# Even mixer: the causal convolution's 31 taps as column-tiled matrix products over shifted copies, with the query and key projection moved to the front

## The chip, the cores and the metric

The kernel runs on one core of one Trainium2 chip. The metric is the device time of one execution in microseconds: 1789.8 us, the median of three runs (1789.62, 1789.8 and 1793.51). The profile below is one execution with a span of 1786.5 us, from its first instruction to its last; 3.3 us lie between that span and the median of the runs.

The core has a matrix engine (PE, with its weight loads shown apart as PEld), two elementwise engines (DVE and ACT), a slow general engine (POOL) and a queue that issues most DMAs (SP). Every engine works through its own list of instructions in order and waits at semaphores for the others.

## The reference

Two stacks of layers run over one sequence of 256 tokens of width 1024. Feed-forward blocks stand around four mixers; the change is inside the first, the even mixer, which runs once:

```python
def even_mixer(h, w_in, w_out, conv_w, conv_b, ln_g, ln_b, q_g, k_g, sinks):
    proj = h @ w_in                              # 256 x 1792
    a_val, a_gate, q, k, v = jnp.split(proj, cuts, axis=-1)   # 512, 512, 512, 128, 128
    u = a_val * jax.nn.sigmoid(a_gate)
    u = lax.conv_general_dilated(u, conv_w[:, None, :], (1,), ((30, 0),), ...,
                                 feature_group_count=512) + conv_b
    u = jax.nn.silu(layer_norm(u, ln_g, ln_b))
    q, k = rms_norm(q, q_g), rms_norm(k, k_g)    # 8 query heads, 2 key heads of 64
    o = banded_attention(q, k, v, 127, sinks)
    return jnp.concatenate([u, o], axis=-1) @ w_out
```

The convolution is causal and depthwise: output t of a channel is the sum over 31 taps of weight k times input t - 30 + k of the same channel. Two tiles of 128 tokens are attended; each channel group j holds 128 of the 512 channels.

## The kernel before, in words

**Weights.** All weights arrive in a fixed list of units (`plan`), each up to 128 x 1024 float32. SP loads unit after unit into six staging buffers. ACT copies a unit to a high part `whi` (L1242), and DVE subtracts to get the low part `wlo` (L1740); there are four buffers of each. A product is then three matmuls, high by high, high by low and low by high (`three`, L596 to L598). SP may load unit u when DVE has split unit u - 6, and ACT may split it when PE has used unit u - 4. A weight unit of the even mixer costs PE 24 matmuls with 256 columns or 12 with 512.

**The even mixer.** Each engine's program is a set of generators that `weave` interleaves: one step of each per round, and each generator starts at its own round. `products` projects and then convolves, `swa` is the attention in turns (turn i issues the scores of pair i of heads, the transposes of pair i - 2 and the value products of pair i - 3), `down` multiplies by `w_out`, and `layer_norm` normalises the convolution's result over the channels (mean, variance and scale go over PE too). The order in each engine's list follows from the starting rounds alone; nothing is reordered at run time.

**The convolution.** 20 of the 31 taps are DVE instructions (L1749, one multiply-add of 128 x 256 per tap and channel group, in `conv`). The other 11 are PE products with diagonal 128 x 128 weights, which ACT writes (L1425). They are plain float32 products of 256 columns (L882), and every such product is two instructions, for the low and the high half of the weights. DVE adds the two sums (L2082). Each channel group's input `ev_u` comes out of a short chain: DVE scales the two projections (L2050), ACT takes a tanh (L1411), DVE combines (L1749).

**Order on PE.** Gate and value columns of groups 0 and 1 first, then queries, keys and values, then groups 2 and 3; then heads are transposed (L784), and 8 steps of taps stand between turns of the attention (scores L842, transposes L829, value products L816). The mean of the normalisation is L917, the transposed attention output L796, the variance L926, the scale row L935. The low half of the normalised part, `ev_ml` (L2130 on DVE), is needed by the fifth of the eight `down` units.

Of the kernel before, what the change touches and what calls it, by code (L numbers as in the profile page):

```python
# [10 lines left out]
ALU = mybir.AluOpType  # L11
# [5 lines left out]
S = 256  # L17
# [9 lines left out]
PE_TAPS = 11  # L27
# [5 lines left out]
def _consts():  # L33
# [29 lines left out]
    put("rcount", np.broadcast_to(rc.reshape(1, -1), (128, 64)))  # L63
    first = np.concatenate(parts, axis=1)
# [139 lines left out]
def build(nc, A, out):  # L204
    ctx = ExitStack()
    with ctx:
# [203 lines left out]
        class Even:  # L410
            def __init__(self, c):
# [8 lines left out]
                self.taps = sb("ev_taps", [128, 4, PE_TAPS, 128], c=c)  # L420
# [8 lines left out]
                self.cwr = sb("ev_cwr", [34, 512], c=c)  # L429
# [3 lines left out]
                self.cw = sb("ev_cw", [128, 4, 34], c=c)  # L433
# [127 lines left out]
        def tensor_program(e):  # L561
# [288 lines left out]
            def even(m):  # L850
# [3 lines left out]
                def products():  # L854
                    for j0 in (0, 2):
                        ps = [room(("ev u", j0 + j)) for j in range(2)]
                        yield from tiles(g, [b[:, 0:256] for b in ps], 256, 4)
                        second = tiles(g, [b[:, 256:512] for b in ps], 256, 4, [("ev u mm", j0)])
                        next(second)
                        yield  # L860
                        next(second)
                        if not j0:
                            row(g)
                        yield
                        for j in range(2):
                            done("ev u", j0 + j)
                        if not j0:
                            heads = x_cols(g, 0, 512)
                            next(heads)
                            conv_weights()  # L870
                            yield
                            yield from heads
                            yield from x_cols(g, 512, 256)

                    for j0 in (0, 2):
                        ps = room(("ev tap", j0))
                        for j in (j0, j0 + 1):
                            e.wait_ge(*K.at("ev u", j))
                            for k in range(PE_TAPS):
                                if k % 6 == 0:  # L880
                                    e.wait_ge(*K.at("ev tap", j, k // 6))
# [3 lines left out]
                                if k + 1 == PE_TAPS and j % 2:  # L885
                                    w.then_inc(*K.inc("tap_mm", ("ev tap mm", j0)))
                                if k % 6 == 5 or k + 1 == PE_TAPS:
                                    yield
                        done("ev tap", j0)

                def conv_weights():
                    ps = room(("ev cw",))
                    e.wait_ge(*K.at("par", g))
                    for j in range(4):
                        w = e.transpose(ps[:, j * 34:(j + 1) * 34], m.cwr[:, j * 128:(j + 1) * 128], ident[0:34, 0:34])
# [43 lines left out]
                weave([(1, products()), (11, swa()), (27, down(g, m.rows)), (24, layer_norm())])  # L939
# [286 lines left out]
        def scalar_program(e):  # L1226
# [172 lines left out]
            def even(m):  # L1399
# [3 lines left out]
                def products():  # L1403
                    for j0 in (0, 2):
# [7 lines left out]
                        if j0:  # L1412
                            return

                        yield from x_cols(512)
                        by_token(g, 0, 512, lambda t: m.qkv[:, t, 0:512].rearrange("p (i j e) -> p j i e", i=4, j=2),
                                 src=lambda ps: ps.rearrange("p (j i e) -> p j i e", j=2, i=4))
                        yield from x_cols(256)
                        by_token(g, 512, 256, lambda t: m.qkv[:, t, 512:768])

                def diagonals():
                    e.wait_ge(*K.at("ev ch"))
                    for j in range(4):
                        for k in range(PE_TAPS):
                            w = e.activation(m.taps[:, j, k, :], ident, ACT.Copy, scale=m.cw[:, j, k:k + 1])  # L1425
                            last = k % 6 == 5 or k + 1 == PE_TAPS
                            w.then_inc(*K.inc("tap", *([("ev tap", j, k // 6)] if last else [])))
                            if last:
                                yield

                def layer_norm():
# [5 lines left out]
                    for j in range(4):  # L1437
                        e.activation(m.sq[:, j, :], m.acc[:, j, :], ACT.Silu, scale=m.cw[:, j, 32:33],
                                     bias=m.cw[:, j, 33:34]).then_inc(*K.inc("ln_silu"))
# [1316 lines left out]
```

## Time and profile before

| | us |
|---|---|
| median of three runs | 1789.8 |
| span of the profiled execution | 1786.5 |
| PE busy | 1772.1 (99%) |
| DVE busy | 1266.1 (71%) |
| ACT busy | 947.8 (53%) |
| even mixer, from its first transpose to the next block's | 190.49 to 297.55, 107.1 |

Busy time is the union of an engine's instructions. PE's instructions overlap (the next one starts before the last one's result is out), so the cost of one in a stream is the distance between starts and not its own duration. "Idle before" is what the engine stood still for, with the instruction that released it.

### The profile page before, as it was taken

Reading aid. Unit: us, or ns where it says so; the run is one execution under the profiler, and the core shown is the slowest. Engines: PE = TensorE matmul, PEld = TensorE weight load, DVE = VectorE, ACT = ScalarE, POOL = GpSimd, SP = SyncE. Lnnn points to the kernel's source line nnn. Section 1 sums busy time; section 2 is a strip of 40 time slices with the busy share of each in tenths; the row PEclk is TensorE's granted clock in tenths of the full one; section 3 lists DMA queues with packets and bytes.
Section 4 is the critical chain, followed back from the end, with each engine's and each line's share of the span. In section 5 each row is a group of like instructions: output and inputs, shape, how many; then the busy total and the mean of one; then the engine's idle time right before and its main releaser. Section 6 shows DMA issues by size and latency. Waiting matters only on the chain.

```text
span 1786.5 us, 24871 instructions
## 1 busy us (share of the span) xinstructions
PE 1772.1 (99%) x9702; PEld 1508.5 (84%) x9702; DVE 1266.1 (71%) x1893; ACT 947.8 (53%) x1348; POOL 30.2 (2%) x39
## 2 busy tenths in 40 slices
PE   9999999999999999999999999999999999999998
PEld 8888888888888888888888788888888878888887
DVE  7774795876577657677656977777755878677774
ACT  6554655554555546555545535455545544555553
POOL 0000000000000001000000000000000000000000
PEclk9999999999999999999999999999999999999999
DMA  8656523666666655466655544556555443456653
GB/s 271 193 180 201 178 72 118 189 177 205 180 193 183 195 177 181 116 196 184 198 169 180 179 130 130 178 181 189 192 193 173 141 155 126 150 188 193 188 195 109
DMA packets 227677, 309.24 MB, mean 173 GB/s; under 512 B 22558, under 2 KB 176318, under 8 KB 227562
## 3 DMA queue, kind: packets, MB, share of 16 engines
q1 hardware_dynamic: 227398, 307.35, 55.1%
q8 instruction: 78, 1.28, 0.3%
q10 hardware_dynamic: 164, 0.30, 0.0%
q14 instruction: 37, 0.30, 0.0%
HBM read 306.57 MB, written 1.05 MB: 172 GB/s over the span
## 4 chain that ended last, share of the span: by engine, by line
PE 92%; DVE 5%; ACT 2%; issue 1%; POOL 0%; POOLq 0%; ACTq 0%; DVEq 0%
PE ps L645 26%; PE ps L596 15%; PE ps L598 15%; PE ps L597 15%; PE ps L647 13%; DVE wlo L1740 1%; PE ps L1144 1%; PE ps L608 1%; PE ps L816 1%; PE ps L842 1%; DVE ev_acc L1749 1%; PE ps L829 1%; ACT whi L1242 1%; PE ps L784 0%; DVE m_scr L1749 0%
## 5 line engine op out<-in xcount | busy, mean ns | idle before, releaser
L1740 DVE TENSOR_TENSOR wlo<-staging,whi 128x1024 fp32r<-128x1024 f32 (+1 forms) x580 | 692.6, 1210 | 339.0 <-ACT whi L1242 338.4
L1242 ACT ACTIVATE whi<-staging 128x1024 fp32r<-128x1024 f32 (+1 forms) x580 | 606.5, 1050 | 477.2 <-PE ps L598 293.7
L645 PE MATMUL ps<-hT,whi 128*128 128x512 f32 x1984 | 624.1, 396 | 0.2 <-DVE wlo L1740 0.2
L647 PEld LDWEIGHTS ps<-hT,wlo 128*128 128x128 f32 x1984 | 372.7, 188 | 88.1
L647 PE MATMUL ps<-hT,wlo 128*128 128x256 f32 x1984 | 389.8, 278 | 0.0
L645 PEld LDWEIGHTS ps<-hT,whi 128*128 128x128 f32 x1984 | 302.1, 189 | 0.4 <-DVE wlo L1740 0.4
L596 PE MATMUL ps<-whi,fh 128*128 128x512 f32 x504 | 196.1, 389 | 0.0
L597 PE MATMUL ps<-wlo,fh 128*128 128x512 f32 x504 | 196.1, 389 | 0.0
L598 PE MATMUL ps<-whi,fl 128*128 128x512 f32 x504 | 196.1, 389 | 0.0
L596 PE MATMUL ps<-whi,hT 128*128 128x512 f32 (+3 forms) x464 | 184.8, 398 | 0.8 <-DVE wlo L1740 0.6
L598 PE MATMUL ps<-whi,hT 128*128 128x512 f32 (+3 forms) x464 | 177.4, 382 | 0.0
L597 PE MATMUL ps<-wlo,hT 128*128 128x512 f32 (+3 forms) x464 | 177.1, 382 | 0.0
L598 PEld LDWEIGHTS ps<-whi,fl 128*128 128x128 f32 x504 | 94.6, 188 | 19.7
L597 PEld LDWEIGHTS ps<-wlo,fh 128*128 128x128 f32 x504 | 94.6, 188 | 19.5
L596 PEld LDWEIGHTS ps<-whi,fh 128*128 128x128 f32 x504 | 94.6, 188 | 19.4
L596 PEld LDWEIGHTS ps<-whi,hT 128*128 128x128 f32 x464 | 87.2, 188 | 21.4 <-issue 3.8
L598 PEld LDWEIGHTS ps<-whi,hT 128*128 128x128 f32 x464 | 87.2, 188 | 16.2
L1313 ACT ACTIVATE fh<-sg 128x512 fp32r<-128x512 f32 x62 | 39.2, 632 | 114.0 <-DVE sg L1844 114.0
L597 PEld LDWEIGHTS ps<-wlo,hT 128*128 128x128 f32 x464 | 87.4, 188 | 14.3 <-issue 0.5
L1829 DVE TENSOR_TENSOR sg<-sg,R 128x512 f32<-128x512 f32 x124 | 85.8, 692 | 4.3
L1826 DVE TENSOR_TENSOR sg<-ps,sg 128x512 f32<-128x512 f32 x124 | 84.8, 684 | 0.2
L596 PE MATMUL ps<-hT,whi 128*128 128x256 f32 x288 | 82.8, 287 | 0.0
(347 smaller groups left out, 1900.6 us busy)
## 6 DMA issues: line engine op xcount, KB each, us to landing
staging<-in_w_in SPq DMA_DIRECT2D x92, 512.0 KB, 3.3
staging<-in_ffn_w_gate SPq DMA_DIRECT2D x84, 512.0 KB, 4.2
staging<-in_ffn_w_up SPq DMA_DIRECT2D x84, 512.0 KB, 4.5
staging<-in_ffn_w_down SPq DMA_DIRECT2D x84, 512.0 KB, 4.1
staging<-in_w_ffn_gate SPq DMA_DIRECT2D x44, 512.0 KB, 4.5
staging<-in_w_ffn_up SPq DMA_DIRECT2D x44, 512.0 KB, 4.6
staging<-in_w_ffn_down SPq DMA_DIRECT2D x44, 512.0 KB, 4.2
staging<-in_od_w_in SPq DMA_DIRECT2D x16, 512.0 KB, 3.7
```

Source lines behind the costliest of these rows:

```text
L596: e.matmul(o, lh, rh, start=start, stop=False)
L597: e.matmul(o, lh, rl, start=False, stop=False)
L598: return e.matmul(o, ll, rh, start=False, stop=stop)
L608: w = e.transpose(ps[:, t * 128:t * 128 + 128], xs[:, t, k * 128:k * 128 + 128], ident)
L645: e.matmul(o, wh[:, kk, j * 128:j * 128 + 128], hT[:, k, :], start=k == 0, stop=False)
L647: m = e.matmul(o[:, 0:256], wl[:, kk, j * 128:j * 128 + 128], hTh[:, k, :], start=False, stop=k == KD - 1)
L816: w = e.matmul(ops[t][:, (h0 + j) * 64:(h0 + j) * 64 + 64], a.pt[i % 2][:, o:o + 128], a.vN(kt, h0 + j), start=kt == 0, stop=kt == t)
L1242: e.activation(high(u)[:, 0:n], stage[u % NS][:, 0:n], ACT.Copy).then_inc(*K.inc("hi", ("hi", u)))
L1313: e.activation(f.fh[:, 2 * p:2 * p + 2, :], s[:, :, 0:256], ACT.Copy).then_inc(*K.inc("fh", ("fh", g, p, 0)))
L1740: e.tensor_tensor(low_of(u)[:, 0:n], stage[u % NS][:, 0:n], high(u)[:, 0:n].bitcast(F32), ALU.subtract).then_inc(*K.inc("lo", ("lo", u)))
L1826: e.tensor_tensor(ss, PS[:, b:b + 2, 0:256], ss, ALU.add).then_inc(*K.inc("ps_r", *[("ev", u) for u in users]))
L1829: e.tensor_tensor(ss, ss, R22, ALU.mult).then_inc(*K.inc("ps_r", ("scaled", g, p, part)))
```

## The change

All 31 taps go to PE, as 8 steps of 4 taps. A product has 32 output channels and contracts over 128 rows: four shifted copies of the 32 channels, stacked on the partitions. Four such products, with 32 columns of weights each, fill the array side by side; each writes its own 32 partitions of the sum. The shifted copies (`u4`) and the weights' taps (`wv`) are laid out by DMAs between SBUF partitions, and DVE multiplies the taps with a constant folded identity to get the weights (`w4`). Queries, keys and values are projected first, so the attention starts at round 7 and lies between the projections of `u` and not between taps only.

```diff
@@ plan_even @@
+            plan_cols(ev, 1024, 512)
+            plan_cols(ev, 1536, 256)
             for c in (0, 256):
                 plan_cols(ev, c, 256)
                 plan_cols(ev, 512 + c, 256)
-                if c == 0:
-                    plan_cols(ev, 1024, 512)
-                    plan_cols(ev, 1536, 256)
@@ PE, products @@
+                    e.wait_ge(*K.at("ev w4"))
                     for j0 in (0, 2):
                         ps = room(("ev tap", j0))
-                        for j in (j0, j0 + 1):
-                            e.wait_ge(*K.at("ev u", j))
-                            for k in range(PE_TAPS):
...
-                                w = e.matmul(ps[:, 256 * (j % 2):256 * (j % 2) + 256], m.taps[:, j, k, :],
-                                             m.u[:, j, PAD - (CONV_W - 1) + k:][:, 0:S], start=k == 0,
-                                             stop=k == PE_TAPS - 1)
+                        e.wait_ge(*K.at("ev u4", j0))
+                        for n in range(2 * STEPS):
+                            j, k = j0 + n // STEPS, n % STEPS
+                            c = 256 * (n // STEPS)
+                            for q in range(GROUPS):
+                                w = e.matmul(ps[32 * q:32 * q + 32, c:c + 256], m.w4[:, q, j, k, :],
+                                             m.u4[:, j, q, 4 * k:4 * k + S], start=k == 0, stop=k == STEPS - 1)
...
+                            if n + 1 in (6, 11, 16):
+                                yield
@@ PE @@
-                weave([(1, products()), (11, swa()), (27, down(g, m.rows)), (24, layer_norm())])
+                weave([(1, products()), (7, swa()), (23, down(g, m.rows)), (22, layer_norm())])
@@ ACT: diagonals() is gone @@
-                            w = e.activation(m.taps[:, j, k, :], ident, ACT.Copy, scale=m.cw[:, j, k:k + 1])
@@ DVE, conv @@
-                        for k in range(PE_TAPS, CONV_W):
...
-                                    w = stt(m.acc[:, j, :], src, m.cw[:, j, k:k + 1], m.acc[:, j, :], ALU.mult, ALU.add)
+                    e.wait_ge(*K.at("ev wv"))
...
+                    for q in range(GROUPS):
+                        e.tensor_tensor(m.w4[:, q, :, :, :].rearrange("p j k c -> p (j k) c"), fold,
+                                        m.wv[:, q, :, :].rearrange("p j k -> p (j k)").unsqueeze(2).broadcast_to(
+                                            [128, 32, 32]), ALU.mult).then_inc(
...
+                            e.tensor_scalar(m.acc[:, j, :], bk("ev tap", j0)[:, c:c + 256], m.cb[:, j, 0:1], None,
+                                            ALU.add).then_inc(
@@ SP @@
+            def taps_load(m):
+                e.wait_ge(*K.at("ev taps"))
+                load("ev_wv", *[(m.wv[quarters[k], q, :, :], m.cwt[quarters[q], k, :, :])
+                                for k in range(GROUPS) for q in range(GROUPS)], steps=[("ev wv",)])
+
+            def shifted_load(m, j0):
+                e.wait_ge(*K.at("ev pad"))
+                e.wait_ge(*K.at("ev u", j0 + 1))
+                n = S + 4 * (STEPS - 1)
+                load(f"ev_u4_{j0}", *[(m.u4[quarters[k], j0:j0 + 2, q, 0:n], m.u[quarters[q], j0:j0 + 2, 1 + k:1 + k + n])
+                                      for k in range(GROUPS) for q in range(GROUPS)], steps=[("ev u4", j0)])
...
+            before = {first[1] + 10: (even_load, evs), first[1] + 14: (taps_load, evs),
+                      first[1] + 18: (shifted_load, evs, 0), first[2]: (shifted_load, evs, 2), first[4] + 10: (odd_load, ods),
```

The list of SP, from the last small parameter of the even mixer to the next block's weights (`ev_w_in` and `ev_w_out` are weight units; `x16` is sixteen DMAs). Before:

```order
L2639 DMA ev_sk<-in_ev_sinks 128x8
L2695 DMA staging<-in_ev_w_in 128x4x256 x4
L2695 DMA staging<-in_ev_w_out 128x1024 x8
L2695 DMA staging<-in_ffn_w_gate 128x4x256 x2
L2695 DMA staging<-in_ffn_w_up 128x4x256 x2
```

Changed:

```order
L2621 DMA ev_sk<-in_ev_sinks 128x8
L2692 DMA staging<-in_ev_w_in 128x4x256 x4
L2621 DMA ev_wv<-ev_cwt 32x32 x16
L2692 DMA staging<-in_ev_w_out 128x1024 x4
L2621 DMA ev_u<-ev_u 32x2x284 x16
L2692 DMA staging<-in_ev_w_out 128x1024 x4
L2621 DMA ev_u<-ev_u 32x2x284 x16
L2692 DMA staging<-in_ffn_w_gate 128x4x256 x2
```

Three batches of sixteen DMAs now stand among the weight units (`ev_u<-ev_u` writes the shifted copies `ev_u4`), and the last two wait for DVE's `ev_u`.

The list of PE at the first taps. `L842` and `L846` are the same line, the attention's scores, before and after. Before:

```order
L882 MATMUL ps<-ev_u,ev_taps 128x256 [waits s_tap,s_ev_u,s_in_act]
L882 MATMUL ps<-ev_u,ev_taps 128x256 x5
L842 MATMUL ps<-ev_kT,ev_qT 128x128 [waits s_in_act,s_heads]
L842 MATMUL ps<-ev_kT,ev_qT 128x128
L882 MATMUL ps<-ev_u,ev_taps 128x256 [waits s_tap]
L882 MATMUL ps<-ev_u,ev_taps 128x256 x4
L842 MATMUL ps<-ev_kT,ev_qT 128x128 [waits s_heads]
```

Changed (value products L820, transposes L833):

```order
L846 MATMUL ps<-ev_kT,ev_qT 128x128 [waits s_pt,s_att_mx]
L846 MATMUL ps<-ev_kT,ev_qT 128x128
L886 MATMUL ps<-ev_u,ev_w 32x256 [waits s_ev_u4_0,s_att_mx,s_conv]
L886 MATMUL ps<-ev_u,ev_w 32x256 x23
L820 MATMUL ps<-ev_qkv,ev 128x64 [waits s_pt]
L820 MATMUL ps<-ev_qkv,ev 128x64
L833 MATMUL ps<-cst,ev 128x128 [waits s_exp,s_att_mx]
L833 MATMUL ps<-cst,ev 128x128
L846 MATMUL ps<-ev_kT,ev_qT 128x256 [waits s_att_mx,s_pt]
L846 MATMUL ps<-ev_kT,ev_qT 128x256
L886 MATMUL ps<-ev_u,ev_w 32x256 x20
```

The first taps stood before the first scores; now they stand behind the scores of turn 3, ahead of those of turn 4, and start with a wait for the first batch of shifted copies. There are six steps of 24, 20, 20, 24, 20 and 20 products.

The list of DVE where the second pair of channel groups is made (`ISA` is the attention's masked score, one pair of heads; a second row of it reads its maximum). Before:

```order
L2021 ISA ev<-ps,cst,ev_skp,ev_hr 128x128 [waits s_att]
L2021 ISA ev 128x1
L2021 ISA ev<-ps,cst,ev_skp,ev_hr 128x128
L2021 ISA ev 128x1
L1749 SCALAR_TENSOR_TENSOR ev_acc<-ev_u,ev_cw,ev_acc 128x256 [waits s_conv] x6
```

Changed:

```order
L1730 TENSOR_TENSOR wlo<-staging,whi 128x1024 [waits s_hi]
L2011 ISA ev<-ps,cst,ev_skp,ev_hr 128x256 [waits s_att]
L2011 ISA ev 128x1
L2011 ISA ev<-ps,cst,ev_skp,ev_hr 128x256
L2011 ISA ev 128x1
L2045 TENSOR_TENSOR ev_th<-ps,R 128x512 [waits s_prod]
L2045 TENSOR_TENSOR ev_th<-ps,R 128x512
L1739 SCALAR_TENSOR_TENSOR ev_u<-ev_th 128x256 [waits s_ev_tanh] x2
L1969 TENSOR_TENSOR ev<-ev 128x8 [waits s_exp]
```

The multiply-adds between the turns are gone, and `ev_u` of groups 2 and 3 now stands behind the masked scores of turn 4 (the first with 256 columns).

## Rows read from the trace of the kernel before

**Rows 1.** The page: busy time, share of the span, instructions.

```profile
PE 1772.1 (99%) x9702; PEld 1508.5 (84%) x9702; DVE 1266.1 (71%) x1893; ACT 947.8 (53%) x1348; POOL 30.2 (2%) x39
```

**Rows 2.** Windows of the even mixer: length, busy time, granted clock, DMA share, GB/s.

```profile
190.50:233.30 42.80, 42.67 (x312) 40.21 (x313) 38.68 (x72) 35.94 (x79) 5.10 (x4) 1.00 0.54 169
233.30:274.70 41.40, 38.86 (x236) 32.00 (x235) 35.72 (x100) 19.19 (x55) 0.00 (x0) 1.00 0.13 39
```

**Rows 3.** What PE waited for, 190 to 298 us: total, times, longest.

```profile
PE ps L816 <- ACT ev L1381: 0.7, 1, 0.7
```

**Rows 4.** Groups by line, DVE, 208 to 266 us: count, busy, mean ns, idle.

```profile
L1749 DVE SCALAR_TENSOR_TENSOR ev_acc<-ev_u,ev_cw,ev_acc 128x256 f32<-128x256 f32 x76 | 31.5, 478 | 0.0
```

**Rows 5.** Groups (first row) and timeline of PE: start, duration, line, operands.

```profile
L882 PE MATMUL ps<-ev_u,ev_taps 128*128 128x256 f32 x88 | 21.0, 387 | 0.0
...
250.40 0.55 PE L816 MATMUL ps<-ev_qkv,ev 128*128 128x64 f32 x4
250.78 0.39 PE L829 MATMUL ps<-cst,ev 128*128 128x128 f32 x2
251.10 0.70 PE L842 MATMUL ps<-ev_kT,ev_qT 64*128 64x256 f32 x4
251.74 2.43 PE L882 MATMUL ps<-ev_u,ev_taps 128*128 128x256 f32 x10
254.00 0.55 PE L816 MATMUL ps<-ev_qkv,ev 128*128 128x64 f32 x4
```

**Rows 6.** Timeline of PE's weight loads: full array, then 32-row tiles.

```profile
233.21 1.12 PEld L784 LDWEIGHTS ps<-cst,ev_qkv 128*128 128x128 f32 x10
...
1016.09 0.52 PEld L1144 LDWEIGHTS ps<-m_scr 32*128 32x128 f32 x8
```

**Rows 7.** Windows: four units of `ev_u` projection, four units of `down`.

```profile
221.79:233.31 11.52, 11.52 (x98) 11.52 (x97) 11.33 (x21) 11.43 (x31) 4.24 (x2) 1.00 0.55 180
...
286.50:297.50 11.00, 10.93 (x48) 9.07 (x49) 7.58 (x8) 4.17 (x4) 0.00 (x0) 1.00 0.89 265
```

**Rows 8.** Timeline of PE, then of DVE: the heads' transposes, and `ev_u`.

```profile
233.31 1.25 PE L784 MATMUL ps<-cst,ev_qkv 128*128 128x128 f32 x10
...
239.47 1.28 DVE L2050 TENSOR_TENSOR ev_th<-ps,R 128x512 f32<-128x512 f32 x2
240.67 0.99 DVE L1749 SCALAR_TENSOR_TENSOR ev_u<-ev_th 128x256 f32<-128x256 f32 x2
```

**Rows 9.** SP's timeline (start, duration of issue), then DMAs: count, size, us to landing.

```profile
200.27 0.60 SPq L2639 DMA_DIRECT2D ev_qg<-in_ev_q_norm_g  x1
214.77 0.34 SPq L2695 DMA_DIRECT2D staging<-in_ev_w_out  x1
...
out<-staging SPq DMA_DIRECT2D x1, 256.0 KB, 2.1
od_qg<-in_od_q_norm_g SPq DMA_DIRECT2D x2, 0.2 KB, 3.5
```

**Rows 10.** Timeline: PE at the end of the attention and normalisation, then DVE.

```profile
268.21 1.89 PE L917 MATMUL ps<-ev_acc,cst 128*128 128x256 f32 x8
272.12 1.06 PE L796 MATMUL ps<-cst,ev_o 128*128 128x128 f32 x8 [1.17 <-DVE ev_o L1996]
273.01 1.84 PE L926 MATMUL ps<-cst,ev_sqc 128*128 128x1 f32 x16
277.55 0.60 PE L935 MATMUL ps<-dg,cst 128*128 128x128 f32 x4
...
285.21 1.22 DVE L2130 TENSOR_TENSOR ev_ml<-ev_sqc,ev_mh 128x1024 fp32r<-128x1024 f32 x1
```

**Rows 11.** Windows after PE's last matmuls, start at 1780.04 and earlier.

```profile
1780.00:1782.00 2.00, 0.43 (x2) 0.01 (x1) 1.81 (x4) 1.12 (x4) 0.00 (x0) 1.00 0.58 238
...
1784.00:1785.00 1.00, 0.00 (x0) 0.00 (x0) 0.00 (x0) 0.00 (x0) 0.00 (x0) 0.81 0.80 299
1785.00:1786.00 1.00, 0.00 (x0) 0.00 (x0) 0.00 (x0) 0.00 (x0) 0.00 (x0) 0.50 0.60 225
```

More of the change, by code:

```diff
@@ L26 @@
 CONV_W = 31
-PE_TAPS = 11
+GROUPS = 4
+STEPS = 8
 PAD = 32
@@ L63, in _consts @@
     put("rcount", np.broadcast_to(rc.reshape(1, -1), (128, 64)))
+    put("fold", np.arange(128)[:, None] % 32 == np.arange(32)[None, :])
     first = np.concatenate(parts, axis=1)
@@ L854, in products @@
                 def products():
+                    heads = x_cols(g, 0, 512)
+                    for _ in range(3):
+                        next(heads)
+                        yield
+                    next(heads)
+                    row(g)
+                    yield
+                    yield from heads
+                    keys = x_cols(g, 512, 256)
+                    next(keys)
+                    conv_weights()
+                    yield
+                    yield from keys
                     for j0 in (0, 2):
@@ L857, in products @@
                         yield from tiles(g, [b[:, 0:256] for b in ps], 256, 4)
[L858 to L864, printed above, removed]
+                        yield from tiles(g, [b[:, 256:512] for b in ps], 256, 4, [("ev u mm", j0)])
                         for j in range(2):
@@ L1458, in swa @@
                     transposed("swa", 4, m.mh[:, 4:8, :])
-                weave([(1, products()), (10, swa()), (6, diagonals()), (27, down(m.rows)), (24, layer_norm())],
-                      catch_up)
+                weave([(1, products()), (6, swa()), (23, down(m.rows)), (22, layer_norm())], catch_up)
             def odd(m):
@@ L2038, in products @@
                 def products():
+                    for n in range(4):
+                        side.due += 1
+                        if n == 1:
+                            diag(g)
+                        if n == 3:
+                            row(g)
+                        yield
+                    conv_weights()
+                    yield from x_cols(256)
                     for j0 in (0, 2):
@@ L2041, in products @@
                             side.due += 1
-                            if half == 1 and not j0:
-                                diag(g)
-                            if half == 3 and not j0:
-                                row(g)
                             yield
@@ L2079, in add_first @@
+                    for j0, rounds in ((0, 5), (2, 3)):
+                        for _ in range(rounds):
+                            yield
                         e.wait_ge(*K.at("ev tap mm", j0))
                         for j in (j0, j0 + 1):
-                            e.wait_ge(*K.at("conv", j, CONV_W - 1))
-                        e.tensor_tensor(m.acc[:, j0:j0 + 2, :], m.acc[:, j0:j0 + 2, :], two(bk("ev tap", j0)),
-                                        ALU.add).then_inc(
-                            *K.inc("conv", ("ev", ("ev tap", j0)), *([("ev conv",)] if j0 else [])))
@@ L2147, in swa @@
                     transposed("swa", 4, m.mh[:, 4:8, :], m.ml[:, 4:8, :])
-                weave([(11, swa()), (1, products()), (5, conv()), (27, down(g, m.rows, 1.0)), (24, layer_norm())],
+                weave([(7, swa()), (1, products()), (9, conv()), (23, down(g, m.rows, 1.0)), (22, layer_norm())],
                       catch_up)
@@ L2651, in even_load @@
                      (m.sk[:, :], A["ev_sinks"].broadcast_to([128, 8])), steps=[("par", m.g)])
+            quarters = [slice(32 * q, 32 * q + 32) for q in range(GROUPS)]
+            def taps_load(m):
[8 more added lines that the diff above has]
+                                      for k in range(GROUPS) for q in range(GROUPS)], steps=[("ev u4", j0)])
             def odd_load(m):
@@ L2711, in sync_program @@
                 if u in before:
-                    stage_load, m = before[u]
-                    stage_load(m)
+                    stage_load, *m = before[u]
+                    stage_load(*m)
                 unit(u)
```

100 lines of the change are left out of this document (34 added, 66 removed).

## The prediction, made before the changed kernel ran

> **What bounds the kernel now.** First the busy times: PE works 99% of the span [rows 1], so only time that PE saves or stands still for can move the end. Then the windows of the even mixer: PE is busy 42.7 of 42.8 us while it projects, and 38.9 of 41.4 us while attention, taps and normalisation alternate [rows 2]. Then the waits: of the idle time in the middle part 0.7 us [rows 3] and 1.2 us [rows 10] have a releaser worth the name, both in the tail of the attention. The changed code therefore has about 2.5 us of idle PE to recover, and everything else must come from cheaper PE work. DVE's 76 multiply-adds, 31.5 us [rows 4], are the largest piece of work that goes, but PE hardly waits for them; nor does it for ACT's weight copies.
>
> **PE work that goes and comes.** A tap step before: ten instructions for five taps of 256 columns start at 251.74, and the next line starts at 254.00 [rows 5]. Of these 2.26 us 0.1 is the first weight load, which nothing hides behind the scores (0.103 us, see [rows 6] below); (2.26 - 0.1) / 10 = 0.216 us each. 88 instructions [rows 5] are 19.0 us.
>
> After: 128 products, 256 instructions of the same 256 columns. What four of them cost when they stand in four column tiles is what the case turns on, and no row shows column tiles. The nearest row is row tiles. Eight loads of 32-row weights, which alternate between two row tiles, take (0.52 - 0.19) / 7 = 0.047 us each; ten loads for the whole array take (1.12 - 0.19) / 9 = 0.103 us each, at the same 128 moving columns [rows 6]. So two tiles do run at once, and that although each product's low and high half follow one another in the list: the second tile's low half starts before the first tile's high half. If column tiles behave alike and all four run at once, the taps are 256 / 4 x 0.216 = 13.8 us. If two run at once they are 27.6 us, if none does 55.3 us. I take four at once, since the nearest row shows as many tiles at once as it has.
>
> A step of another tile shape than its neighbour's costs PE a drain: the scores' four instructions last from 251.10 to 251.74 where two overlapping pairs of 0.216 us would be 0.43 [rows 5], 0.2 us for going in. I give each of the six tap steps 0.3 us, 1.8 us in all. PE work then changes by -19.0 + 13.8 + 1.8 = **-3.4 us**.
>
> The Trainium skill, in "TensorE: Matmul & The Clock Gate", part 3 "Packing small matmuls", gives a measured 2.38 times for three column tiles, says that matmuls start and end strictly in the order of the list, and that a weight load is pulled ahead of running matmuls only when the row group differs. Rows 6 speak against the strict order, for row tiles. By that rule a column tile's high half would hold back the next tile's low half, and only two products would overlap, as in the second rival below.
>
> **When the first shifted copies are there.** The product units are the same ones, only their order changes; before, the last of them ends at 233.3 [rows 7]. Now the transposes of the heads (234.40 - 233.31 = 1.1 us, [rows 8]), four scores of 0.42 (the row's 0.63 is for twice the columns), two transposes of 0.32 and a value product of 0.39 [rows 5] lie in front of that point: PE reaches the first tap at 233.3 + 3.8 = 237.1. The last unit for groups 0 and 1 ends four units earlier (11.5 us, [rows 7]), at 221.8. Behind it come the transposes of the heads 1.1, one unit 2.9 and the first scores 0.4: 226.2. DVE's list then has a low part, two masked scores (0.7) and `ev_u` (239.47 to 241.66, 2.2 us [rows 8]); with the low part's wait for ACT I come to 229.7.
>
> SP then issues sixteen DMAs. One small DMA among others takes 0.60 us to issue, one large one that stands alone 0.34 [rows 9]; with 0.04 between them that bounds a batch of sixteen (fifteen distances) by 5.7 and 9.6 us. I take 0.55 each, nearer to the small ones: 8.3 us. From the last issue to landing are 2.1 to 3.5 us [rows 9]; I take the middle, 2.8. Copies: 229.7 + 8.3 + 2.8 = 240.8, and PE stands still from 237.1 for **3.7 us**. The batch of tap weights before it is issued while DVE still has its old work, and PE does not wait for it.
>
> **When the second ones are there.** This is a chain through four queues. `ev_u` of groups 2 and 3 stands on DVE behind the masked scores of turn 4, which PE issues only behind the first tap step: 240.8 + 24 products (6 x 0.43 + 0.3 = 2.9) + value product, transposes and scores (1.3) = 245.0; masked scores 1.1 and `ev_u` 2.2 = 248.3; sixteen DMAs 8.3 and 2.8 = 259.4. On PE lie two tap steps of 2.45, three pieces of attention of 1.3 to 1.6, and 1.6 us of waiting for ACT, whose copy and exponentials stand behind the tanh: PE is there at 254.4 and stands still for **5.0 us**.
>
> **The tail.** From 259.4: three tap steps 2.9 + 2.45 + 2.45, attention between them 2.0 + 1.4 + 1.4, to 272.0; the last value product with ACT's copy before it (0.7, as in [rows 3]) 1.8; the output's scaling and transposes 1.7, as 0.8 and 0.9 ([rows 10], 272.12 to 273.01); the mean 1.7: 277.2, where the first `down` unit starts. Before, the last taps end at 262.2 and the variance, which now comes one unit later, ends at 274.7 [rows 10]. Unit 2.7, variance 1.7, unit 2.7: the scale row starts at 284.3. From it to the end of `ev_ml` were 286.4 - 277.55 = 8.9 us [rows 10] over DVE, ACT and DVE again. Three `down` units (8.2 us) covered that; now only two (5.4 us) do, because `layer_norm` starts one round before `down` and not three rounds. `ev_ml` is there at 293.2, a wait of **3.4 us** for PE in place of 0.3. Four more units of 2.73 [rows 7] end the mixer at 304.1, against 297.55.
>
> **The sum.** -3.4 us of work, +3.7, +5.0 and +3.1 of new waits, and small ones that cancel (1.6 for ACT behind the tanh, less 2.5 of idle time that goes with the old order; the walk's own rest is -0.9): +6.6 us. Outside the mixer nothing changes; the units of the next block are loaded long before. The profiled execution would have a span of 1786.5 + 6.6 = 1793.1, and with the 3.3 us between span and median the time is **1796.4 us**.
>
> **The rivals.**
>
> *Two products at a time.* For it: the list's order, low and high half of one tile behind each other, and that no row shows more than two tiles at once. The first tap step grows by 2.5 us, and so does the second batch's arrival; the next two hide in the wait that is there anyway; the last three grow by 6.7. Together +6.6 + 2.5 + 6.7 = +15.8: 1805.6 us.
>
> *None at a time.* For it: rows 6 are row tiles, another direction of the array. 55.3 us of taps, of which the second wait's 5.0 us hide nearly all: +6.6 + (55.3 - 13.8) - 5.0 - 2 = +41: 1831 us.
>
> *Not slower.* Its one mechanism is the speed of the two batches of DMAs between SBUF partitions. At 0.34 + 0.04 us an issue and 2.1 us to land, the copies come at 237.5 and, down the same chain, at 252.6. PE waits 0.4 and 1.7 us instead of 3.7 and 5.0, and the end moves by -6.8: 1789.6 us. The sum turns at about 0.38 us an issue. Against it: the small DMAs of the same queue took 0.60 [rows 9]. If the tap steps also cost less to enter than I say and the waits for ACT go with DVE's lighter list, it would be 1784.
>
> *The clock falls in a wait.* PE's granted clock was 1.00 until 1784 and 0.50 from 1785 on, with no matmul since 1780.4: it fell after some 4 us of idle [rows 11], from 2.4 to 1.2 GHz. The waits of 3.7 and 5.0 us are of that size. Every microsecond of taps behind them that runs at the lower level takes two: with a step and its attention (4.2 us) behind each wait, up to +8, I take +4: 1800 us. [...]
>
> **How the numbers follow.** A difference of under 0.3% (5.4 us) counts as no change. Four at a time 0.44: 1796.4, own range 1790 to 1802, of which 0.27 is slower and 0.17 the same. Two at a time 0.25, none 0.06, the clock on top of four at a time 0.05: all slower. Not slower 0.20, of which 0.08 the same and 0.12 faster. Slower 0.63, same 0.25, faster 0.12. The range leaves out the case of none (0.06), the half of "not slower" that gains most and the upper end of two at a time: 1786 to 1812 holds about 0.83.
>
> **What would show it.** The group of tap products: 256 instructions; in a step of 24 products the starts of a round of four lie 0.43 us apart if four run at once, 0.86 if two do, 1.7 if none. PE's waits must name the two DMAs of shifted copies, with 3 to 4 and about 5 us, and DVE's `ev_ml` with about 3 us. SP's rows must show sixteen issues in about 9 us, twice, the second starting 18 to 20 us after the first. DVE's time falls by some 25 us without any effect on the end. The windows between the waits must show a granted clock of 1.00. The forecast is wrong if PE waits under 2 us for both batches together, if a round of four costs more than 0.6 us, or if PE's idle time shows up at the projections, where the tap weights' batch holds SP and DVE.

## The result and the profile after

The changed kernel takes **1805.1 us** (median of 4 runs, 1804.2 to 1805.9), the kernel before 1789.7 (4 runs): 1.0087 times as long, 95% interval 1.0075 to 1.0099. The forecast was 1796.4 with a range of 1786 to 1812. The sign and the range held; of the 15.4 us, the likeliest case had only 6.6.

The mixer itself, from one normalisation's first transpose to the next one's. Timeline of TensorE, before and after (start, duration, line, operands):

```profile
190.49 0.74 PE L608 MATMUL ps<-cst,xs 128*128 128x128 f32 x5
...
297.55 0.71 PE L608 MATMUL ps<-cst,xs 128*128 128x128 f32 x5
```

```profile
192.07 1.07 PE L612 MATMUL ps<-cst,xs 128*128 128x128 f32 x8
...
315.15 1.03 PE L612 MATMUL ps<-cst,xs 128*128 128x128 f32 x8
```

107.06 us became 123.08: **+16.0 us**. The other 1.5 us between the spans (1786.5 and 1804.0) lie ahead of the mixer, where the two programs are the same. There the granted clock of TensorE was low for a while in this execution and stood at 1.00 over the same four microseconds in the kernel before (window, all engines, of the changed kernel):

```profile
9.00:13.00 4.00, 3.61 (x17) 3.47 (x18) 3.80 (x6) 3.64 (x9) 0.00 (x0) 0.57 1.10 368
```

The traces of runs 4, 6, 9 and 10 below have the same low stretch, the others don't, so times of two kernels can differ by some 1.5 us that no edit made. All that the change itself does is in these 123 us. What TensorE waited for there (total, times, longest), where before only two were worth the name, 0.7 us [rows 3] and 1.2 us [rows 10]:

```profile
PE ps L886 <- DMA ev_u<-ev_u: 10.3, 2, 6.2
PE ps L600 <- DVE ev_ml L2111: 3.0, 1, 3.0
PE ps L820 <- ACT ev L1385: 1.4, 2, 0.8
PE ps L800 <- DVE ev_o L1986: 0.9, 1, 0.9
```

The three waits of the forecast are there: for the first and the second copies, and for `ev_ml`. What the rows of waits don't show is what came behind them. The timeline of the six tap steps (48 instructions are 24 products, 40 are 20):

```profile
243.32 5.13 PE L886 MATMUL ps<-ev_u,ev_w 128*32 128x256 f32 x48 [4.14 <-DMA ev_u<-ev_u]
249.83 2.37 PE L886 MATMUL ps<-ev_u,ev_w 128*32 128x256 f32 x40
...
265.00 4.53 PE L886 MATMUL ps<-ev_u,ev_w 128*32 128x256 f32 x48 [6.20 <-DMA ev_u<-ev_u]
271.58 2.37 PE L886 MATMUL ps<-ev_u,ev_w 128*32 128x256 f32 x40
```

Undisturbed, 40 instructions last 2.30 us from their first start to the next line's, and 48 last 2.73 (in runs 1 and 8 below), so six rounds cost 0.43 us more than five: a round of four products costs 0.43 us, as one product did before [rows 5], and going into a step costs 0.14. The steps behind the two waits took 5.06 and 4.46 us by the same measure. The windows of TensorE (length, busy time, granted clock, DMA share, GB/s) say why:

```profile
241.00:243.00 2.00, 0.00 (x0) 0.57 0.47 115
243.00:248.00 5.00, 4.68 (x45) 0.50 0.99 366
...
249.00:250.00 1.00, 1.00 (x11) 1.00 0.00 0
...
265.00:268.00 3.00, 3.00 (x30) 0.50 0.99 327
268.00:269.00 1.00, 1.00 (x20) 0.71 0.15 43
270.00:272.00 2.00, 2.00 (x22) 1.00 0.00 0
282.00:285.00 3.00, 3.00 (x12) 0.54 0.00 0
303.00:306.00 3.00, 3.00 (x8) 0.50 0.78 232
```

The granted clock fell from 1.00 to 0.50 (2.4 to 1.2 GHz) four times, and not once in the mixer before [rows 2]: in both waits for copies, in the attention's tail, and in the wait for `ev_ml`. Note also the DMA share of 0.99 in the same windows: what made the steps slow is not settled by these rows alone.

And the chain, behind which the second wait stands (start, duration, what):

```profile
241.09 2.09 DMA ev_u<-ev_u
243.32 5.13 PE ps L886 x48
248.45 0.59 PE ps L820 x4
249.04 0.23 PE ps L833 x2
249.26 0.66 PE ps L846 x4
249.95 1.02 DVE ev L2011 x4
250.97 1.21 DVE ev_th L2045 x2
252.20 0.43 ACT ev_th L1420
252.65 0.44 DVE ev_u L1739
253.15 0.60 SPq L2621
...
262.74 2.13 DMA ev_u<-ev_u
265.00 4.53 PE ps L886 x48
```

It is the chain of the forecast, link by link: copies, first step, scores, masked scores, `ev_u`, sixteen issues, landing. So whatever lengthens the first step also delays the second batch. The issues (min, median and max in ns behind the count, then the first and the last start) follow one another 0.64 us apart. The first batch takes 10.2 us and the second 9.6, and not 8.3:

```profile
L2621 SPq DMA_DIRECT2D ev_u<-ev_u x32: 596/597/1106, 230.9 to 262.7; - x32
```

### The profile page after: what moved, and what is told of

Read it like the earlier page. It is cut to its first block, busy times and chain, and to the rows that moved or that the text cites. A ratio compares the mean times of both kernels' runs of the same rounds, so it can differ in the third digit from the quotient of the medians.

```text
span 1804.0 us, 25136 instructions
## 1 busy us (share of the span) xinstructions
PE 1775.9 (98%) x9870; PEld 1505.8 (83%) x9870; DVE 1241.2 (69%) x1819; ACT 935.4 (52%) x1304; POOL 30.3 (2%) x40
## 4 chain that ended last, share of the span: by engine, by line
PE 93%; DVE 3%; SPq 1%; ACT 1%; issue 1%; DMA 1%; POOLq 0%; POOL 0%; ACTq 0%; DVEq 0%
PE ps L649 26%; PE ps L600 16%; PE ps L602 15%; PE ps L601 15%; PE ps L651 13%; PE ps L612 1%; PE ps L1148 1%; SPq L2621 1%; PE ps L820 1%; DVE wlo L1730 1%; PE ps L846 1%; PE ps L886 1%; PE ps L833 1%; PE ps L788 1%; DVE m_scr L1739 0%
```

## The experiments

Eleven runs, all variants of the changed kernel, timed against the kernel before on the same chip (1788.6 to 1789.5 us there). The changed kernel's own 1805.1 us was taken once, beside 1789.7, so a difference to it is one across chips; the mixer's length in the trace, taken as above, is the finer measure. The numbers in brackets are the range of the runs, the ratio to the kernel before, and its 95% interval.

### 1. TensorE kept busy in the waits

```
  ps = room(("ev tap", j0))
+ for _ in range(13 if j0 else 9):
+     e.matmul(ps[:, 0:256], C("ones"), cst[:, 0:256], start=True, stop=True)
  e.wait_ge(*K.at("ev u4", j0))
```

> Ahead of the two waits for the shifted copies TensorE multiplies constants into the bank that the taps then overwrite: 9 products of 256 columns (18 instructions at 0.216 us, 3.9 us) ahead of the first, 13 (5.6 us) ahead of the second. The copies can land no sooner by it. Theory A (the waits of 4.2 and 6.2 us drop the granted clock to 0.5 and the first tap step behind each runs at the lower level): the granted clock stays 1.00 from 238 to 272 us, both first steps of 48 instructions take 2.75 us in place of 5.06 and 4.46, and what follows the second batch is as far behind it as before: 2.3 + 1.7 = 4.0 us less, 1801. Theory B (those two steps are slow for another reason: the share of the DMA engines, at 1.0 just then, slows TensorE's reads of SBUF, or the first round of taps is slow by itself): 48 instructions still take 4.5 to 5 us, and the time stays at 1805 or rises by what the fillers run over.

Measured: 1799.3 us (1797.9 to 1802.2; 1.0056, interval 1.0041 to 1.0071), the mixer 117.3 us. Timeline of the two steps, and the windows that hold them:

```profile
241.23 2.80 PE L888 MATMUL ps<-ev_u,ev_w 128*32 128x256 f32 x48
...
260.48 2.80 PE L888 MATMUL ps<-ev_u,ev_w 128*32 128x256 f32 x48 [0.31 <-DMA ev_u<-ev_u]
```

```profile
241.00:244.00 3.00, 2.93 (x50) 1.00 0.89 317
256.00:260.00 4.00, 4.00 (x20) 1.00 0.47 114
260.00:264.00 4.00, 3.69 (x56) 1.00 0.86 265
```

Theory A. Both steps fall by 2.33 and 1.73 us, with the DMA share nearly as high as before (0.89 and 0.86 in place of 0.99): the clock made them slow, not the traffic. Work that computes nothing made the kernel 5.8 us faster. 4.1 of these are the two steps; the rest, some 1.7 us, is in the tail, where the mean's eight instructions now took 1.54 us and not 2.65: here the clock stayed up, though the tail's waits of 0.7 and 0.9 us were the same. Behind the wait for `ev_ml`, where nothing filled in, it fell as before.

### 2. Nobody waits for the copies

```
- e.wait_ge(*K.at("ev u4", j0))
+ e.wait_ge(*K.at("ev pad"))
+ e.wait_ge(*K.at("ev u", j0 + 1))
- ... m.u4[:, j, q, 4 * k:4 * k + S], ...
+ ... m.u[:, j, 4 * k:4 * k + S], ...
```

> The tap products read ev_u itself where they read its shifted copies, so they wait only for ev_u; all 32 copies are still issued, and nobody waits for them. It leaves out the shift of the three other taps of each product. Theory A (the loss lies in the two waits for DMAs and the clock that they cost): the waits of 4.2 and 6.2 us and the slow steps (2.3 and 1.7 us) go, 14.4 us in all: 1791. What stays against the kernel before is then the wait for ev_ml with its own fall of the clock, 3.0 and 1.8 us, the same in the tail, 1.4 us, less 3.4 us of cheaper taps. Theory B (the new order of the projections is dear by itself, since attention now alternates with the u products and has no cover later): the waits move to DVE's masked scores and ACT's exponentials, and the time is above 1797.

Measured: 1789.0 us (10 runs, 1787.3 to 1790.0; 0.9999, interval 0.9990 to 1.0008). Theory A: the two waits and what hangs on them are nearly the whole slowdown. By time it is 16.1 us; by the mixer, which shrinks from 123.1 to 108.5, it is 14.6, where 14.4 were expected, and the other 1.5 us lie at the start of the program. The 3.0 us for `ev_ml` and the lower clock in the tail and behind it stay, and the cheaper taps balance them but for 1.4 us. No new wait of size shows that the order of the projections costs anything by itself.

### 3. Tile by tile

```
- for q in range(GROUPS):                      # k outside: tiles alternate
+ for i in range(GROUPS * n, GROUPS * n + GROUPS):
+     half, q, k = i // 32, i // STEPS % GROUPS, i % STEPS   # tile outside
```

> The same 128 tap products, but the eight steps of one column tile follow one another (tile outermost) where the four tiles alternated. Theory A (neighbours in the list run at once only if they stand in different column tiles): a product costs its whole 0.43 us, and the taps 128 x 0.43 = 55 us in place of 14.7. The first step grows by 7.5 us, the next two by 12.4 of which the second wait takes up 6.2, the last three by 20, less some 2 for a clock that no longer falls in a second wait: +31 us, 1836. Theory B (TensorE looks far enough ahead to fill the idle tiles from further down the list, or the tiles never were what made it fast): a step stays at 2.3 to 3 us and the time at 1805.

Measured: 1825.3 us (1825.2 to 1825.6; 1.0199, interval 1.0184 to 1.0214): slower than with alternating tiles by 20.2 us, where 31 were expected. Timeline of the steps at full clock:

```profile
254.76 7.15 PE L886 MATMUL ps<-ev_u,ev_w 128*32 128x256 f32 x40
263.29 7.15 PE L886 MATMUL ps<-ev_u,ev_w 128*32 128x256 f32 x40
272.04 8.88 PE L886 MATMUL ps<-ev_u,ev_w 128*32 128x256 f32 x48
```

Four products more cost 1.73 us, 0.43 each: neighbours in the same tile do follow one another. But 20 products would be 8.6 us and took 7.08, 24 would be 10.4 and took 8.81. Both steps change tiles twice, and each change saves 0.8 us, the time of two products. In the trace instructions follow 0.216 us apart until, 6 ns after the thirteenth of the sixteen of a tile, one more starts: the next tile's first. Four of either then run side by side. So theory A holds for neighbours, and B is right in that TensorE looks ahead, by about two products. The twelve changes of tile save 9.6 us, and that is most of the 11 us that the expectation missed; the other 1.7 us are the tail, which ran at the full clock here.

### 4. The projections in the old order

```
  plan, TensorE, ScalarE, VectorE: u (0, 1), heads, keys, u (2, 3), as before
- if n + 1 in (6, 11, 16): yield
+ if n % 4 == 3: yield
- weave([(1, products()), (7, swa()), (23, down(...)), (22, layer_norm())])
+ weave([(1, products()), (11, swa()), (27, down(...)), (24, layer_norm())])
```

> The new taps, but with the projections in the order of the kernel before (u of groups 0 and 1, heads, keys, u of groups 2 and 3), attention four rounds later as before, and the taps in eight steps of 16 products. Theory A (the copies' delay is what costs, not the tap products): the first copies land some 5 us before TensorE wants them; the second u is there at about 236, its copies at 236 + 16 x 0.64 + 2.1 = 248.3, and TensorE is there at about 245: one wait of 3 to 4 us, at most a short fall of the clock behind it. With 3.4 us of cheaper taps and the usual three rounds between mean and the first W_out product, so that ev_ml is not waited for: 1790, within 1787 to 1794. Theory B (taps in column tiles cost more than they save, or alternate badly with attention): above 1797 whatever the order.

Measured: 1798.3 us (1797.2 to 1801.5; 1.0046, interval 1.0029 to 1.0062). Neither theory: it is 8 us above A, and though the time is B's, the tap products didn't cost more. In the trace, which is of the slowest of the four executions, TensorE waited 6.7 us for the second copies and 4.1 us for `ev_qkv`, the scaled keys. The chain that ends in the keys:

```profile
232.57 0.60 SPq L2624
233.21 4.52 DMA staging<-in_ev_w_out
237.76 1.06 ACT whi L1247
238.85 1.23 DVE wlo L1734
240.07 0.34 DVE ev_qkv L2125
```

I had counted what the sixteen issues hand over late, and not what stands behind them in SyncE's list. A load of `W_out` weights goes out when the batch is done, at 233.2; its splitting stands on ScalarE and VectorE ahead of the keys' scaling, although the keys have nothing to do with it; and TensorE waits for the keys. `ev_u` of groups 2 and 3 was done at 248.4 and not at about 236, since it stood behind masked scores that waited for TensorE.

### 5 to 7. One cause at a time

```
e5  - for k in range(GROUPS) for q in range(GROUPS)]   (SyncE)
    + for k in range(2) for q in range(GROUPS)]        (SyncE), k = 2, 3 on GpSimd, behind its head norms
e6  - weave([(7, swa()), (1, products()), (9, conv()), ...        (VectorE)
    + weave([(1, products()), (7, swa()), (9, conv()), ...
e7  - (22, layer_norm())      on TensorE, ScalarE, VectorE; conv's rounds (0, 5), (2, 3)
    + (20, layer_norm())                                                 (0, 5), (2, 2)
```

> Of each sixteen DMAs of shifted copies SyncE issues eight and GpSimd, which has nothing else to do then, the other eight. Theory A (the copies are late because one queue needs 0.64 us for each of sixteen issues): if GpSimd issues as fast, a batch is issued in 5.1 us, the first copies are there at 230.9 + 5.1 + 2.1 = 238.1, before TensorE wants them, so the wait of 4.2 us goes and with it the slow first step, 2.3 us. The second batch is shorter by 5.1 us: 1.1 us of its 6.2 us stay, too short for the clock to fall, which gives 1.7 us more. 13.3 us less than 1805.1: 1792. Theory B (GpSimd needs twice as long for an issue, or the landing of the copies is what takes long): at 1.3 us an issue nothing is gained, 1805, and above it more is lost.

Measured: 1791.1 us (10 runs, 1790.4 to 1793.1; 1.0010, interval 1.0001 to 1.0019). The first wait is gone, of the second 1.4 us are left, and the clock stays up in the taps and in the tail. It falls behind `ev_ml`, where it now costs 2.9 us in place of 1.7. The mixer takes 109.7 us, 13.3 less, as expected. GpSimd issues one every 0.53 us (rows as for SyncE above):

```profile
L2590 POOL DMA_DIRECT2D ev_u<-ev_u x16: 536/536/712, 229.5 to 248.7; - x16
```

> Only VectorE's order changes: in each round what belongs to the products (the low part, the scaling of u) stands ahead of attention's masked scores, so ev_u of groups 2 and 3 no longer waits for the scores that TensorE issues behind the first tap step. Theory A (that order is why the second batch is late): u is there at 238.0 + 2.7 = 240.7; SyncE ends the first batch at 241.7, issues four loads of weights (2 us) and then the second, which lands at 243.8 + 10.2 + 2.1 = 256.1; TensorE wants it at 258.1. The wait of 6.2 us and the slow step behind it (1.7 us) go, the first wait of 4.2 us stays: 1797. Theory B (the second batch is bound by something else, the queue or the landing): the wait only shrinks by the 2 to 3 us between the two batches, 1802, or the scores come later and attention pays: 1805.

Measured: 1794.6 us (1793.5 to 1796.2; 1.0030, interval 1.0019 to 1.0042). The second wait is gone, and its slow step; of the two waits for copies one is left:

```profile
242.70 5.35 PE L886 MATMUL ps<-ev_u,ev_w 128*32 128x256 f32 x48 [3.73 <-DMA ev_u<-ev_u]
...
257.16 2.80 PE L886 MATMUL ps<-ev_u,ev_w 128*32 128x256 f32 x48
```

> The layer norm starts two rounds earlier (round 20, three before W_out's first product, as in the kernel before), so the mean stands ahead of the last value product and the scale row one unit earlier. Theory A (ev_ml was waited for since only two units lay between scale row and its first use): three units, 8.2 us, cover 8.9 us of DVE and ACT: the wait of 3.0 us shrinks to 0.7 and the clock does not fall behind it (1.8 us); the mean's products also fill the wait for ACT's last exponentials, up to 1.4 us. 5.5 us less: 1799.6. Theory B (the mean or the variance now wait themselves, for the taps' bias on DVE and the squares on ACT): the wait moves and at most 2 us are gained, 1803 or more.

Measured: 1799.6 us (1798.7 to 1801.3; 1.0057, interval 1.0044 to 1.0071). `ev_ml` costs 0.2 us in place of 3.0, the clock doesn't fall behind it, and TensorE's waits for ACT and DVE in the attention go from 2.5 to 2.1 us.

Theory A in all three runs, with 0.9 us under, 2.4 us under and 0.0 us off the time expected. That the last one met its time to the tenth is in part luck: in its trace the first wait was 0.6 us longer than in the changed kernel, and the two slow steps together 1.2 us shorter (4.3 and 4.1 us).

### 8. All three

> The changed kernel with all three edits of the last runs: two queues, the second u earlier, the mean earlier. Theory A (the loss is nothing but the two waits for the copies, the wait for ev_ml and the clock behind the three; the taps themselves are 3 to 4 us cheaper than before): the run in which nobody waited for copies took 1789.0, and the earlier mean takes 5.5 us off that: 1783.5, within 1782 to 1786, faster than the kernel before (1789.5). Theory B (the edits compete: GpSimd and SyncE issue at the same time, VectorE's square, bias and masked scores crowd in the last rounds): 1788 or more.

Measured: **1783.8 us** (6 runs, 1782.5 to 1785.8; 0.9970, interval 0.9958 to 0.9982): faster than both. Timeline of the mixer's ends, then all that TensorE waited for in it, then two windows:

```profile
190.39 0.84 PE L612 MATMUL ps<-cst,xs 128*128 128x128 f32 x6
...
291.43 0.82 PE L612 MATMUL ps<-cst,xs 128*128 128x128 f32 x6
```

```profile
PE ps L800 <- DVE ev_o L1987: 1.2, 1, 1.2
PE ps L887 <- DMA ev_u<-ev_u: 0.4, 1, 0.4
PE ps L600 <- DVE ev_ml L2112: 0.2, 1, 0.2
```

```profile
237.00:275.00 38.00, 36.42 (x403) 1.00 0.33 107
275.00:291.00 16.00, 15.76 (x70) 1.00 0.60 177
```

The mixer takes 101.0 us, 6.0 less than before and 22.0 less than in the changed kernel, with the same 256 tap instructions. The granted clock is 1.00 in all of it. That may not be so in each execution: run 7's trace has the same wait of 1.2 us for `ev_o`, and there the clock fell behind it and cost 1.6 us.

### 9 and 11. The old order of projections with the queues mended

e9 is e4 with the edits of e5 and e6. e11 moves GpSimd's first eight issues ahead of the head norms.

> The projections in the old order with the new taps once more (1798.3 in the run before), with the two queues and VectorE's order (u ahead of the masked scores). In that run's trace TensorE waited 4.1 us for the keys, since SyncE issued a batch of copies until 233.2 us and W_out's loads, whose splitting stands ahead of the keys on ScalarE and VectorE, came only then; and 6.7 us for the second copies. Theory A (both waits come from SyncE's sixteen issues and VectorE's order, not from the order of the projections): W_out's loads go out 5 us sooner, the keys' wait shrinks to 1 us or none; the second copies are issued from 239 on and land at 246, before TensorE wants them; the two steps at the lower clock (3.57 in place of 1.87 us) go: 3.1 + 6.7 + 3.4 = 13.2 us less, 1785. Theory B (with u first attention has less cover, whatever the queues do): the keys' wait stays over 3 us or attention's waits grow in the tail: 1790 or more.

Measured: 1789.8 us (10 runs, 1787.9 to 1794.0; 1.0004, interval 0.9995 to 1.0014), which is B's time within 0.2 us but not its place. The keys' wait is gone, the second copies are in time, but now the first ones are late by 4.1 us: in GpSimd's list they stand behind the square root for the keys.

> As the last run with u first (1789.8, a wait of 4.1 us for the first copies), but GpSimd issues its eight first copies ahead of the square roots of the head norms and not behind them. In the trace of that run its list held them back: the root for the keys ended at 234.4, eight issues until 238.2, landing at 240.1. Theory A (that list is all that was left): the issues start at 223 with ev_u, the copies are there by 231, the wait of 4.1 us and the lower clock behind it (0.6 us in the first, 0.7 us in the second step) go: 1784.4, as fast as the other order with its three edits (1783.8). Theory B (the roots are now late in turn: they wait behind eight issues of 0.53 us, and heads and keys with them): the wait moves to the transposes of the heads and over 2 us of the 5.4 stay: 1786.5 or more.

Measured: 1787.9 us (10 runs, 1786.1 to 1791.6; 0.9997, interval 0.9987 to 1.0007). The first wait is gone and 2.2 us of waiting for the second copies have come in its place, with a step at the lower clock behind it:

```profile
PE ps L888 <- DMA ev_u<-ev_u: 2.2, 1, 2.2
```

Theory B's time, but not its place: nothing moved to the heads. I don't count the old order as worse by nature. As far as it was taken it does as well as the kernel before and some 4 us worse than the new order with its edits, and each repair brought up the next wait.

### 10. One tile of four

```
- for q in range(GROUPS):
+ for q in range(1):
```

> The changed kernel with only one of the four products of each tap round, 32 products in place of 128; it leaves out three quarters of the convolution. Theory A (four column tiles run wholly at once): a round of one product takes as long as one of four, 0.43 us, and the steps keep their 2.3 and 2.7 us; the time stays at 1805, within 2 us. Theory B (the four share something, the issue of instructions or the reading of moving columns, so that the round of eight instructions is bound by 8 x 0.054): a round of two instructions is shorter, down to 0.11 us, the first and the last three steps shrink by up to 7 us in all, and the time falls to 1798 or less.

Measured: 1804.3 us (1803.8 to 1805.6; 1.0082, interval 1.0065 to 1.0099). Timeline:

```profile
254.69 2.35 PE L886 MATMUL ps<-ev_u,ev_w 128*32 128x256 f32 x10
```

10 instructions last as long (2.35) as the 40 of the changed kernel (2.37), and with three quarters of the tap products gone the mixer is as long as in the changed kernel (123.1 us). Three of four products are free: four column tiles run wholly at once.

## Why the prediction was partly right

**Point by point.** Mixer, predicted and measured:

| Term | Predicted | Measured |
|---|---|---|
| a round of four products | 0.43 us | 0.43 us |
| going into a tap step | 0.3 us | 0.14 us |
| tap work | -3.4 (19.0 to 15.6) | -5.3 (19.9 to 14.6) |
| wait for the first copies | +3.7 | +4.1 |
| wait for the second copies | +5.0 | +6.2 |
| wait for `ev_ml` (0.3 before) | +3.1 | +2.7 |
| lower clock | 0 | +7.4 |
| small ones | -1.8 | +0.9 (the rest) |
| sum | +6.6 | +16.0 |

The lower clock is 2.3 and 1.7 us in the two steps, 0.6 and 1.1 us in the tail (the output's transposes took 1.47 in place of 0.90 us, the mean 2.65 in place of 1.54, against run 1), and 1.7 us behind `ev_ml` (nine instructions in 3.71 us, where 0.23 each would be 2.04).

The taps after are 2 x 2.73 + 4 x 2.30 = 14.6 us at the full clock. Before, the eight steps were about 4 x 2.70 + 4 x 2.27 = 19.9 us by the same measure. The forecast's 19.0 left out what going into each of them costs (0.1 us) and counted it for the new steps, so its saving was 0.9 us too small for that alone.

**The step that failed is the term for the clock**, which the forecast put at 0 in the likeliest case and at 4 us in a rival with a chance of 0.05. It had the row for it: the clock fell after some 4 us without a matmul at the end of the span [rows 11]. Three terms of its own sum were waits of 3.1 to 5.0 us. With such rows, the fall belonged to the likeliest case and the steady clock to the rival. It also asked only what runs slowly behind a wait for copies and passed over the wait for `ev_ml` and the tail. Run 1 shows the two steps' part by itself, 4.1 us. The 1.7 us of the tail also went in that run, but they went without an edit in run 5 too, so they are not the fillers' doing for certain.

The Trainium skill says in "TensorE: Matmul & The Clock Gate", part 1, that an idle engine loses the full clock and has to work before it gets it back. The waits of this trace agree: in the first one the clock was at 0.50 by 242 us, and it was back at 1.00 by 249, after 5 us of tap products.

**Smaller misses.** The small terms were off by 2.7 us. TensorE's waits for ACT and DVE, without `ev_ml`, are 2.6 us where they were 2.5: the old order's idle time, which the forecast let go, was still there in the tail, and the wait behind the tanh (1.0 us, forecast 1.6) came on top. The remaining -0.9 was a rest of the walk without a cause of its own, and the trace doesn't have it. Two of the forecast's signs also failed: the second batch started 22 us after the first and not 18 to 20, and the windows between the waits show a clock of 0.50 until 248.

**A rival had the time and not the cause.** "Two products at a time" gave 1805.6, 0.5 us from the measured 1805.1. Its sign was a round of 0.86 us. The round took 0.43, and run 10 shows that four products cost what one does. Had only the time been looked at, the wrong rival would have been taken for shown. The range held with luck, too: its upper end was there for this rival and not for the clock, whose own rival ended at 1800.

The Trainium skill gives in "TensorE: Matmul & The Clock Gate", part 3, 2.38 times for three column tiles and a strict order of starts. Here it is four times for four (run 10). The starts in the trace of the changed kernel come in fours, 6 to 7 ns apart, and the next four 0.2 us later. Run 3 shows instructions of one tile 0.216 us apart, so each four must be in four tiles: the low halves start ahead of the high halves that stand between them in the list. What the opening says, that nothing is reordered at run time, holds for the lists and not for the starts within TensorE.

**What held:** the chain through four queues, with 0.64 us from one issue to the next where I took 0.55 (the row of the small DMA was the right one [rows 9], and one issue of 1.1 us took the first batch beyond its bound of 9.6, to 10.2) and 2.1 us to landing where I took 2.8; and that nothing outside the mixer changes. VectorE's busy time fell by 24.9 us (1266.1 to 1241.2), as forecast, and the kernel got slower; what the relief is worth by itself no run tests. The remark that `ev_ml` lost a covering unit is shown by run 7, and the two waits by runs 2, 5 and 6.

**What stays open:** why the clock fell in the tail in some traces and not in others. With the same waits of 0.7 and 0.9 us there it fell in the changed kernel and in runs 2, 6 and 10, and not in runs 1, 3 and 5. With a wait of 1.2 us it fell in runs 7 and 9, and not in runs 4, 8 and 11 or in the kernel before. And whether the old order of projections, rid of all its waits, would be faster still.

## What to carry to other kernels

When a change adds a wait for TensorE of several microseconds, cost the wait and the clock behind it together, and look for small waits that follow; here they were 13.0 us and 7.4. A batch of small DMAs costs its queue an issue each (here 0.64 us, sixteen of them 9.6 to 10.2) and holds up all that stands behind it in that engine's list: spread it over queues that are idle, and follow what it delays to those that have nothing to do with it. And a time that comes out as forecast does not show the cause; look for the sign in the trace.

## What the runs showed of the hardware

- Four matmuls with 32-column weights, each in a column tile of its own, take the time of one: 0.43 us a round of eight instructions and also a round of two (run 10).
- TensorE starts instructions of another column tile ahead of the list's order, but only some: with eight products of one tile behind each other, four instructions of the next were taken early, 0.8 us saved at each change of tile (run 3).
- GpSimd issued a DMA of the same size every 0.53 us where SyncE needed 0.64. With both at it SyncE's eight issues took 5.2 to 5.8 us, where eight at 0.64 are 5.1; from issue to landing the median went from 2.1 to 2.7 us on SyncE's queue (run 5).
- Products that compute nothing, put into two waits, held the clock at 1.00 there and took 4.1 us off the two steps behind them; the kernel got 5.8 us faster in all (run 1).
